# Moving a third of a head's value projection behind the sample products of the head before, and the store of V behind the copies of the keys

## The chip, the cores and the metric

The kernel runs on one core of a Trainium2 chip. The metric is the device time of one execution in microseconds, the median of several runs. The core's engines work side by side and meet at semaphores: TensorE (PE) multiplies matrices, VectorE (DVE) and ScalarE (ACT) do elementwise work, GpSimd (POOL) prepares weights, SyncE (SP) issues the transfers of weights. ACT issues transfers too.

## The reference, cut to what matters

One inference step of a two-layer trunk over a prompt of 1024 tokens and 8 sample tokens, 1032 columns in all. Layer 0 is a Mamba-2 mixer and a squared-ReLU MLP. From its output, keys and values are projected once, for 8 heads; layer 1 is differential attention over them and another MLP. For the sample tokens the attention also looks at 256 cached positions in pages. The part that the change touches, per head:

```python
kv = h @ w_kv
k = rope(kv[..., :QK_WIDTH_B].reshape(bt, l, N_HEADS_B, 2, HEAD_DIM_B), pos)
v = kv[..., QK_WIDTH_B:].reshape(bt, l, N_HEADS_B, 2 * HEAD_DIM_B)
# of a sample token: two softmaxes over 256 cached positions and its own, combined
w = (p[:, :, 0] - lam * p[:, :, 1]).astype(v_new.dtype)
o = einsum('bhqk,bkhe->bqhe', w[..., :lp], v_past) + einsum('bhqk,bkhe->bqhe', w[..., lp:], v_new)
o = rms_norm(o, subln_g) * (1.0 - lam_init)
return o.reshape(bt, l, V_WIDTH_B) @ w_o
```

Keys and values of all heads are outputs as well, and are stored from SBUF as they are (`kT`, `vT`).

## The kernel before

**Tiling.** Activations lie transposed: 128 partitions of features by 1032 columns of tokens, cut into NCH = 3 chunks of CW = 344 columns. A weight unit is 128 x 1024; SP loads it, POOL splits it into a high and a low part (`wh`, `wl`), and a product is the sum of three matmuls (high by high, high by low, low by high) so as to keep fp32 precision. One chunk of a projection over 1024 features is thus 8 x 3 = 24 matmuls of 344 columns (`chunk_of`, line 323), into one of three banks of `jb`. A bank is given back through `bank_free`, a filled bank is announced through `chunk_full`.

**The attention in passes.** `project_head(at, n, new, fin)` is written once for each engine and does two things interleaved: it begins head n (`new`: rotary queries and keys, projection of V) and ends head p = n - 1 (`fin`: the sample tokens' attention, the normalisation, the output projection by `w_o`). `attend(n)` then does the prompt's attention of head n and, between its steps, projects the queries and keys of head n + 1. Pass 0 only begins, passes 1 to 7 do both, pass 8 only ends. The order within a pass is written out by hand for each engine; nothing plans it.

**PE in a pass** (line numbers of the profile): broadcast of the sample queries (580), turn of the queries by `perm` (572), chunk 0 of V (323), sample scores transposed (590, 592), chunk 1 of V, then, after `rope_done`, turn of the keys by `perm` (572), chunk 2 of V. Then the sample tokens: after `sp_ready` the weights are spread over partitions (605, 606), after `wsm_ready` come 32 products of the cached values with one column each (612), which raise `so_full`. Then, after `osq_done`, the sums of squares over each column (377, `rms_sums`), after `raw_v` the transposes of V (622), after `orms_inv` the spread of the reciprocal roots (385, `rms_spread`), and after `a_lo` the output projection of head p (323 again, 8 jobs of 3 chunks of 3 matmuls).

**ACT in a pass**: high halves of the queries (981), exponential of the sample scores (984), the three chunks of V copied from `jb` to `raw` (`take`, 770), a drain that raises `raw_v`, the store of V (992), high halves of the keys (995), the square of `ob` (998, raises `osq_done`), copies of the key halves to the other partitions by transfers (`twin`, 970), the store of the keys (1002), the copies of the low halves (970 again, after DVE's `k_low`), the root (1007), the high part of V (1010), the high part of the output (1014).

**DVE in a pass**: sample scores (1453, 1460), rotary queries (1421 to 1426), softmax of the sample scores (1466 to 1478, raises `sp_ready`; 1481 raises `wsm_ready`), rotary keys, the sample output (1489, after `so_full`, raises `o_smp`), low halves of the keys (1439), V's sample columns (1496, after `raw_v`), the reciprocal of the root (1182), the normalisation (1503), low parts (1510, 1513), and the accumulation of the output projection (1132).

The scores of a head (655) wait until all its key copies have landed (`k_twin`). The next write into `raw` waits for the stores (`v_out`, `k_out`) in `attend`.

Of the kernel before, what the change touches and what calls it, by code (L numbers as in the profile page):

```python
# [28 lines left out]
ACT = mybir.ActivationFunctionType  # L29
# [6 lines left out]
T = SEQ + NB  # L36
NCH = 3
CW = T // NCH
KD = D // P
# [45 lines left out]
def half_of(m):  # L85

    return slice(HD * m, HD * m + HD)
# [23 lines left out]
def program(nc, a, o):  # L111
    with ExitStack() as ctx:
        def sb(name, shape, dt=F32, into=None):
            return (into or ctx).enter_context(nc.sbuf_tensor(name, shape, dt))
# [5 lines left out]
        xh = sb("xh", [P, KD, T], F32R)  # L120
        xl = sb("xl", [P, KD, T], F32R)
# [70 lines left out]
        raw = sb("raw", [P, T], F32, m)  # L192
# [60 lines left out]
        s = {n: sem(n) for n in names}  # L253
# [59 lines left out]
        def _(pe):  # L313
            mm = nc.tensor.matmul

            def chunk_of(place, c, j, kt, rh, rlo):

                slot, credits, _ = place
                pe.wait_ge(bank_free[c], credits)
                cols = slice(c * CW, (c + 1) * CW)  # L320
                for k in range(kt):
                    for w, x, p in ((wh, rh, 0), (wh, rlo, 1), (wl, rh, 2)):
                        last = mm(jb[:, c, 0:CW], w[slot][:, j * kt + k], x[:, k, cols],  # L323
                                  start=(k == 0 and p == 0), stop=(k == kt - 1 and p == 2))
                        if c == 0 and j == 0 and k == 0 and p == 0:
                            last.then_inc(unit_begun, 1)
                last.then_inc(chunk_full, 1)
# [247 lines left out]
            def project_head(at, n, new, fin):  # L575

                p = n - 1
                if fin:
                    for b in range(NB):
                        last = mm(aux[:, b // 4, (b % 4) * 128:(b % 4) * 128 + 128],  # L580
                                  smp[:, 0, b:b + 1].to_broadcast([P, P]), ident[:], start=True, stop=True)
                    last.then_inc(s["qb_full"], 1)
                if new:
                    perm_of(2 * n + 1, raw)
                    vp = (unit(at), *at.job())
                    chunk_of(vp, 0, 0, KD, xh, xl)
                if fin:

                    pe.wait_ge(s["ssc_ready"], p + 1)
                    mm(aux[0:16, 0, 256:257], qkn[:].rearrange("p m b -> p (m b)"), one[:], start=True, stop=True)  # L590
                    for g in range(PAGES):
                        last = nc.tensor.transpose(aux[0:16, 0, g * 128:(g + 1) * 128],
                                                   ssc[:, g].rearrange("p m b -> p (m b)"), ident[:])
                    last.then_inc(s["srow_full"], 1)
                if new:
                    chunk_of(vp, 1, 0, KD, xh, xl)

                    pe.wait_ge(s["rope_done"], 2 * n + 1)
                    perm_of(2 * n + 2, raw_k)
                    chunk_of(vp, 2, 0, KD, xh, xl)  # L600
                if fin:

                    pe.wait_ge(s["sp_ready"], p + 1)
                    for g in range(PAGES):
                        mm(aux[:, 1, g * 8:g * 8 + 8], srow[0:16, g * 128:(g + 1) * 128], pair[0:16, 0:8], start=True, stop=True)
                    mm(aux[:, 1, 16:24], srow[0:16, 256:257].to_broadcast([16, P]), pair[0:16, 0:8], start=True,
                       stop=True).then_inc(s["wsm_full"], 1)
                    pe.wait_ge(s["wsm_ready"], p + 1)
                    pe.wait_ge(s["pv_in"], 16 * p + 16)
                    for b in range(NB):  # L610
                        for g in range(PAGES):
                            last = mm(aux[:, 1, 32 + b:33 + b], past[:, b * PAGES + g], wsm[:, g, b:b + 1],
                                      start=(g == 0), stop=(g == PAGES - 1))
                    last.then_inc(s["so_full"], 1)
                if fin:
                    rms_sums(p, "orms_full", "osq_done", pp, 1)
                if new:

                    pe.wait_ge(s["raw_v"], n + 1)
                    pe.wait_ge(s["rope_done"], 2 * n + 2)  # L620
                    for c in range(8):
                        last = nc.tensor.transpose(aux[:, 3 + c // 4, (c % 4) * 128:(c % 4) * 128 + 128],
                                                   raw[:, c * 128:(c + 1) * 128], ident[:])
                    last.then_inc(s["vt_ps"], 1)
                if fin:
                    rms_spread(p, "orms_scale", "orms_inv")
                if fin:
                    slot = unit(at)
                    place = (slot, *at.job())
                    for c in range(NCH):  # L630
                        pe.wait_ge(s["a_lo"], 3 * p + c + 1)
                        chunk_of(place, c, 0, 1, ah, al)
                    for j in range(1, KD):
                        place = (slot, *at.job())
                        for c in range(NCH):
                            chunk_of(place, c, j, 1, ah, al)
# [93 lines left out]
        def _(act):  # L730
# [36 lines left out]
            def take(c, done, dst, func, **kw):  # L767

                act.wait_ge(chunk_full, done + c + 1)
                af(dst, jb[:, c, 0:CW], func, **kw).then_inc(bank_free[c], 1)  # L770
# [201 lines left out]
            def project_head(at, n, new, fin):  # L972
                p = n - 1
                if fin:

                    act.wait_ge(s["ssc_ready"], p + 1)
                    act.dma_start(past[:], vgat[:, :, bass.ds(p * P, P)].rearrange("g t d -> t g d")).then_inc(s["pv_in"], 16)
                if new:
                    act.wait_ge(s["rope_done"], 2 * n + 1)
                    for m_ in range(2):  # L980
                        af(q2[m_][half_of(m_)], rot[half_of(m_), 0:SEQ], ACT.Copy).then_inc(s["qk_hi"], 1)
                if fin:
                    act.wait_ge(s["snm_ready"], p + 1)
                    af(srow[0:16, 0:257], srow[0:16, 0:257], ACT.Exp, scale=SCALE, bias=st[0:16, 4:5],
                       accum_out=st[0:16, 5:6]).then_inc(s["sexp_ready"], 1)
                if new:
                    _, done = at.job()
                    for c in range(NCH):
                        take(c, done, raw[:, c * CW:(c + 1) * CW], ACT.Copy)
                    act.drain().then_inc(s["raw_v"], 1)  # L990
                    act.wait_ge(s["raw_v"], n + 1)
                    act.dma_start(o["vT"][:, bass.ds(n, 1)].rearrange("p a t -> p (a t)"), raw[:]).then_inc(s["v_out"], 16)
                    act.wait_ge(s["rope_done"], 2 * n + 2)
                    for m_ in range(2):
                        af(k2h[m_][half_of(m_)], rot[half_of(m_), 0:SEQ], ACT.Copy).then_inc(s["qk_hi"], 1)
                if fin:
                    act.wait_ge(s["o_smp"], p + 1)
                    af(pp[:, 0:T], ob[:], ACT.Square).then_inc(s["osq_done"], 1)
                if new:
                    act.wait_ge(s["qk_hi"], 4 * n + 4)  # L1000
                    twin(k2h)
                    act.dma_start(o["kT"][:, bass.ds(n, 1)].rearrange("p a t -> p (a t)"), rot[:]).then_inc(s["k_out"], 16)
                    act.wait_ge(s["k_low"], 2 * n + 2)
                    twin(k2l)
                if fin:
                    act.wait_ge(s["orms_full"], p + 1)
                    af(rstd[:, 0], aux[:, 0, 0:9], ACT.Sqrt, bias=eps[:]).then_inc(s["orms_sqrt"], 1)
                if new:
                    act.wait_ge(s["vt_ps"], n + 1)
                    af(vth[:], aux[:, 3:5].rearrange("p a (b c) -> p (a b) c", b=4), ACT.Copy).then_inc(s["vt_hi"], 1)  # L1010
                if fin:
                    for c in range(NCH):
                        act.wait_ge(s["on_ready"], 3 * p + c + 1)
                        af(ah[:, 0, c * CW:(c + 1) * CW], ob[:, c * CW:(c + 1) * CW], ACT.Copy).then_inc(s["a_hi"], 1)
                    at.job(8)
# [43 lines left out]
            _, done = at.job(2)  # L1059
# [687 lines left out]
```

## Time and profile before

| what | value |
|---|---|
| median of 3 runs | 3885.5 us (3884.25 to 3893.59) |
| span of the profiled execution | 3857.8 us |
| busy in the span | PE 89%, DVE 59%, ACT 25%, POOL 26% |
| mean granted clock of TensorE in the span | 0.922 |
| attention, passes 0 to 8 | about 2085 to 3025 us of the span |

The span runs from the first to the last instruction; the device time of a run also holds what lies around it. The granted clock is TensorE's: 1.00 is 2.4 GHz, 0.50 is 1.2 GHz, and a mean between them is a mixture of the two. A row of the timeline tells start, duration, engine, line, operation, tiles and count of merged instructions, and in brackets the idle time before and what ended it. ACTq is ACT's sequencer, which issues transfers. PE's matmuls are pipelined: the start-to-start distance is the pace, the duration of one is longer.

### The profile page before, as it was taken

What the parts mean: (1) busy time and instruction counts of PE and PEld (TensorE: products, weight loads), DVE (VectorE), ACT (ScalarE), POOL (GpSimd) and SP (SyncE); (2) the same over time, 40 slices, a digit from 0 to 9 for tenths busy, and PEclk for the clock granted to TensorE, in tenths of its full rate; (3) what the DMA queues carried; (4) which work ended last, traced back from release to release, by engine and by line L of the source; (5) the groups of instructions that cost most, each with busy time, mean ns of one, the idle gap of its engine ahead of it and who ended that gap; (6) DMA issues with size and microseconds to landing.
All of it is one profiled execution on the core that took longest, in us unless ns stands there. A gap on an engine that the chain in (4) does not pass through costs nothing.

```text
span 3857.8 us, 55382 instructions
## 1 busy us (share of the span) xinstructions
PE 3440.0 (89%) x21050; PEld 3288.6 (85%) x21050; DVE 2287.6 (59%) x3463; ACT 953.7 (25%) x2235; POOL 1011.1 (26%) x455
## 2 busy tenths in 40 slices
PE   6888988889887899999997888888886799999997
PEld 6788888888787899999996787777775799999997
DVE  6677777777776834343457666666675753333335
ACT  3333333233332311111103323222322211111112
POOL 3123132222221233343431111111110043333331
PEclk9899999999998899999997888888897699999997
DMA  4231111111110011111112111211111011111111
GB/s 165 74 110 57 46 44 42 51 39 45 43 48 34 28 44 46 49 45 50 44 50 63 59 35 49 65 60 60 60 41 41 11 50 45 45 50 44 45 48 52
DMA packets 85936, 200.29 MB, mean 52 GB/s; under 512 B 8920, under 2 KB 46808, under 8 KB 85248
## 3 DMA queue, kind: packets, MB, share of 16 engines
q1 hardware_dynamic: 35552, 139.54, 10.8%
q10 hardware_dynamic: 50224, 58.37, 4.9%
q8 instruction: 131, 2.15, 0.2%
q14 instruction: 29, 0.24, 0.0%
HBM read 166.93 MB, written 39.60 MB: 54 GB/s over the span
## 4 chain that ended last, share of the span: by engine, by line
issue 65%; PE 19%; POOLq 9%; POOL 5%; SPq 1%; DVE 0%; ACT 0%; DMA 0%; ACTq 0%; DVEq 0%
PE jb L323 18%; POOLq L298 8%; POOL wl L299 5%; SPq L273 1%; PE aux L499 0%; DMA wraw<-in_wstream 0%; ACT acc L907 0%; DVE acc L1316 0%; POOLq L306 0%; POOLq L295 0%; SPq L263 0%; SPq L269 0%; DVE lnq L1320 0%; ACT lnq L895 0%; PE aux L506 0%
## 5 line engine op out<-in xcount | busy, mean ns | idle before, releaser
L296 POOL TENSOR_TENSOR wh<-wraw,one 128x1024 fp32r<-128x1024 f32 x225 | 444.5, 1976 | 2749.5 <-PE jb L323 2275.8
L323 PE MATMUL jb<-xh,wh 128*128 128x344 f32 x2784 | 912.7, 328 | 45.9 <-issue 18.6
L323 PE MATMUL jb<-xl,wh 128*128 128x344 f32 x2784 | 899.0, 323 | 0.0
L323 PE MATMUL jb<-xh,wl 128*128 128x344 f32 x2784 | 898.1, 323 | 0.0
L1132 DVE TENSOR_TENSOR acc<-jb,acc 128x344 f32<-128x344 f32 x672 | 332.1, 514 | 457.0 <-PE jb L323 446.3
L323 PEld LDWEIGHTS jb<-xh,wh 128*128 128x128 f32 x2784 | 532.0, 191 | 54.1 <-issue 22.8
L299 POOL TENSOR_TENSOR wl<-wraw,wh 128x1024 fp32r<-128x1024 f32 x225 | 566.3, 2517 | 32.0
L323 PEld LDWEIGHTS jb<-xl,wh 128*128 128x128 f32 x2784 | 531.5, 191 | 1.6
L323 PEld LDWEIGHTS jb<-xh,wl 128*128 128x128 f32 x2784 | 531.2, 191 | 0.0
L323 PE MATMUL jb<-hh,wh 128*128 128x344 f32 x1536 | 492.3, 321 | 0.0
L323 PE MATMUL jb<-hl,wh 128*128 128x344 f32 x1536 | 491.0, 320 | 0.0
L323 PE MATMUL jb<-hh,wl 128*128 128x344 f32 x1536 | 490.5, 319 | 0.0
L1373 DVE TENSOR_TENSOR rl<-rl 128x344 f32<-128x344 f32 x192 | 158.1, 823 | 371.7 <-ACT hh L944 371.5
L942 ACT ACTIVATE rl<-jb 128x344 f32<-128x344 f32 x192 | 87.8, 457 | 1072.7 <-PE jb L323 1045.7
L323 PEld LDWEIGHTS jb<-hh,wh 128*128 128x128 f32 x1536 | 288.8, 188 | 3.4 <-DVE acc L1132 3.4
L323 PEld LDWEIGHTS jb<-hh,wl 128*128 128x128 f32 x1536 | 288.6, 188 | 0.0
L323 PEld LDWEIGHTS jb<-hl,wh 128*128 128x128 f32 x1536 | 288.1, 188 | 0.0
L1375 DVE TENSOR_TENSOR hl<-rl,hh 128x344 fp32r<-128x344 f32 x192 | 228.4, 1190 | 15.8 <-issue 2.0
L1163 DVE SCALAR_TENSOR_TENSOR ct<-pre,pg,ct 128x1024 f32<-128x1024 f32 x96 | 165.3, 1722 | 99.4 <-ACT cnew L813 90.6
L323 PE MATMUL jb<-yh,wh 128*128 128x344 f32 x384 | 136.8, 356 | 69.0 <-DVE acc L1132 51.7
L1034 ACT ACTIVATE pp<-aux,st 128x256 f32<-128x256 f32 (+7 forms) x128 | 94.1, 739 | 280.4 <-PE jb L666 158.1
L323 PEld LDWEIGHTS jb<-yh,wh 128*128 128x128 f32 x384 | 79.2, 206 | 79.5 <-DVE acc L1132 60.2
(247 smaller groups left out, 5662.9 us busy)
## 6 DMA issues: line engine op xcount, KB each, us to landing
wraw<-in_wstream SPq DMA_DIRECT2D x225, 512.0 KB, 3.3
kgat<-in_cache_k SPq DMA_DIRECT2D x16, 512.0 KB, 5.2
vgat<-in_cache_v SPq DMA_DIRECT2D x16, 512.0 KB, 6.1
pre<-in_state ACTq DMA_DIRECT2D x16, 512.0 KB, 4.2
out_ssm_s<-pre ACTq DMA_DIRECT2D x16, 512.0 KB, 3.5
past<-kgat ACTq DMA_DIRECT2D x8, 1024.0 KB, 5.9
past<-vgat ACTq DMA_DIRECT2D x8, 1024.0 KB, 5.9
acc<-in_xT SPq DMA_DIRECT2D x8, 516.0 KB, 7.0
```

Source lines behind the costliest of these rows:

```text
L273: pages = [sp.value_load(a["ptab"][0:1, k:k + 1], min_val=0, max_val=PHYS - 1) for k in range(NB * PAGES)]
L296: nc.gpsimd.tensor_tensor(wh[slot][:].rearrange("p k m -> p (k m)"), wraw[:, slot].rearrange("p k m -> p (k m)"), one[:].to_broadcast([P, ...
L298: pool.drain()
L299: nc.gpsimd.tensor_tensor(wl[slot][:], wraw[:, slot], wh[slot][:].bitcast(F32), ALU.subtract).then_inc(w_split, 1)
L323: last = mm(jb[:, c, 0:CW], w[slot][:, j * kt + k], x[:, k, cols], start=(k == 0 and p == 0), stop=(k == kt - 1 and p == 2))
L942: af(rl[:, x % 4], jb[:, x % 3, 0:CW], ACT.Relu).then_inc(bank_free[x % 3], 1)
L1034: af(pp[:, m_ * 1024:m_ * 1024 + width], src, ACT.Exp, scale=SCALE, bias=st[:, m_:m_ + 1], accum_out=st[:, 2 + m_:3 + m_]).then_inc(s["p_r ...
L1132: tt(acc[:, k, cols], jb[:, c, 0:CW], acc[:, k, cols], ALU.add).then_inc(bank_free[c], 1)
L1163: stt(ct[:, 0:SEQ], src[:, 1 + k:1 + k + SEQ], w(k), ct[:, 0:SEQ], ALU.mult, ALU.add)
L1373: tt(rl[:, x % 4], rl[:, x % 4], rl[:, x % 4], ALU.mult)
L1375: tt(hl[b][:, j, cols], rl[:, x % 4], f(hh[b][:, j, cols]), ALU.subtract).then_inc(s["h_ready"], 1)
```

## The change

In `project_head` of PE, chunk 2 of V moves from behind the turn of the keys to behind the sample products, ahead of the sums of squares. In `project_head` of ACT, two chunks of V are taken at the old place; the third take, the drain that raises `raw_v` and the store of V move behind the copies of the key's high halves and the store of the keys, ahead of the copies of the low halves. DVE, POOL and SP are unchanged, and the number of instructions is the same. In pass 0, which has no sample products, PE's order stays as it is, and only ACT's changes; pass 8 does not change.

```diff
@@ PE, project_head
                     pe.wait_ge(s["rope_done"], 2 * n + 1)
                     perm_of(2 * n + 2, raw_k)
-                    chunk_of(vp, 2, 0, KD, xh, xl)
                 if fin:
                     pe.wait_ge(s["sp_ready"], p + 1)
...
                     last.then_inc(s["so_full"], 1)
+                if new:
+                    chunk_of(vp, 2, 0, KD, xh, xl)
                 if fin:
                     rms_sums(p, "orms_full", "osq_done", pp, 1)
@@ ACT, project_head
                     _, done = at.job()
-                    for c in range(NCH):
+                    for c in (0, 1):
                         take(c, done, raw[:, c * CW:(c + 1) * CW], ACT.Copy)
-                    act.drain().then_inc(s["raw_v"], 1)
-                    act.wait_ge(s["raw_v"], n + 1)
-                    act.dma_start(o["vT"][:, bass.ds(n, 1)].rearrange("p a t -> p (a t)"), raw[:]).then_inc(s["v_out"], 16)
                     act.wait_ge(s["rope_done"], 2 * n + 2)
...
                     act.wait_ge(s["qk_hi"], 4 * n + 4)
                     twin(k2h)
                     act.dma_start(o["kT"][:, bass.ds(n, 1)].rearrange("p a t -> p (a t)"), rot[:]).then_inc(s["k_out"], 16)
+                    take(2, done, raw[:, 2 * CW:T], ACT.Copy)
+                    act.drain().then_inc(s["raw_v"], 1)
+                    act.wait_ge(s["raw_v"], n + 1)
+                    act.dma_start(o["vT"][:, bass.ds(n, 1)].rearrange("p a t -> p (a t)"), raw[:]).then_inc(s["v_out"], 16)
                     act.wait_ge(s["k_low"], 2 * n + 2)
                     twin(k2l)
```

## Rows read from the trace of the kernel before

**Rows 1.** The page: busy time by engine, and granted clock in 40 slices.
```profile
PE 3440.0 (89%) x21050; PEld 3288.6 (85%) x21050; DVE 2287.6 (59%) x3463; ACT 953.7 (25%) x2235; POOL 1011.1 (26%) x455
...
PEclk9899999999998899999997888888897699999997
```

**Rows 2.** Passes by stretch: length, busy PE, PEld, DVE, ACT, POOL, granted clock, DMA, GB/s.
```profile
2187.70:2307.30 119.60, 101.55 (x574) 93.61 (x575) 76.28 (x134) 33.81 (x72) 17.19 (x8) 0.83 0.18 53
...
2652.50:2765.20 112.70, 95.85 (x575) 88.29 (x575) 75.89 (x134) 33.87 (x72) 17.22 (x8) 0.89 0.18 56
```

**Rows 3.** Timeline of PE in pass 4: start, us, engine, line, operation, count, idle before.
```profile
2539.80 2.00 PE L572 MATMUL aux<-raw_k,perm 128*128 128x344 f32 x6 [0.56 <-DVEq L1427]
...
2542.11 0.32 PE L323 MATMUL jb<-xh,wh 128*128 128x344 f32 x1
...
2545.25 0.32 PE L323 MATMUL jb<-xh,wl 128*128 128x344 f32 x1
2545.50 0.61 PE L605 MATMUL aux<-pair,pp 16*128 16x8 f32 x4
...
2546.72 4.20 PE L612 MATMUL aux<-ssc,past 128*128 128x1 f32 x32 [0.40 <-DVEq L1482]
2554.18 4.00 PE L377 MATMUL aux<-ones,pp 128*128 128x1 f32 x18 [3.26 <-ACT pp L998]
...
2559.80 3.90 PE L385 MATMUL aux<-ident,rstd 128*128 128x128 f32 x18
```

**Rows 4.** Stretches of pass 4, columns as in rows 2.
```profile
2545.50:2549.80 4.30, 3.90 (x35) 3.82 (x34) 3.00 (x5) 0.46 (x1) 0.00 (x0) 1.00 0.30 123
2549.80:2554.20 4.40, 1.14 (x7) 1.05 (x7) 2.51 (x4) 3.17 (x3) 0.00 (x0) 0.50 0.00 0
...
2559.70:2563.40 3.70, 3.70 (x19) 3.60 (x18) 0.02 (x1) 1.02 (x1) 0.00 (x0) 0.50 0.05 13
```

**Rows 5.** Timeline of DVE in pass 4, columns as in rows 3.
```profile
2544.62 0.40 DVE L1478 TENSOR_SCALAR pp<-pp,st,pair 16x257 f32<-16x257 f32 x1
...
2551.21 0.17 DVE L1489 TENSOR_TENSOR ob<-aux,smp 128x8 f32<-128x8 f32 x1
...
2563.74 1.54 DVE L1503 SCALAR_TENSOR_TENSOR ob<-ob,subg,aux 128x344 f32<-128x344 f32 x3 [4.02 <-PE aux L385]
```

**Rows 6.** Timeline of ACT and its transfer issues in pass 4.
```profile
2545.61 0.46 ACT L770 ACTIVATE raw<-jb 128x344 f32<-128x344 f32 x1 [2.48 <-PE jb L323]
2546.36 0.37 ACTq L992 DMA_DIRECT2D out_vT<-raw  x1
...
2553.07 1.12 ACTq L970 DMA_DIRECT2D k2h<-k2h  x2
2554.29 0.55 ACTq L1002 DMA_DIRECT2D out_kT<-rot  x1
2555.58 2.30 ACTq L970 DMA_DIRECT2D k2l<-k2l  x2
2557.91 1.28 ACT L1007 ACT_TABLE_LOAD   x1 [3.78 <-issue]
2559.21 0.27 ACT L1007 ACTIVATE rstd<-aux,eps 128x9 f32<-128x9 f32 x1
```

**Rows 7.** Pass 8: PE's products in the timeline, and their stretch.
```profile
2989.90 6.95 PE L612 MATMUL aux<-ssc,past 128*128 128x1 f32 x32 [1.11 <-DMA past<-vgat]
...
2990.00:2997.00 7.00, 6.85 (x32) 6.77 (x32) 0.11 (x1) 0.00 (x0) 0.00 (x0) 0.50 0.01 2
```

**Rows 8.** Timeline of PE: matmuls of the output projection of pass 4.
```profile
2567.07 0.49 PE L323 MATMUL jb<-ah,wl 128*128 128x344 f32 x1
...
2567.93 0.49 PE L323 MATMUL jb<-ah,wl 128*128 128x344 f32 x1
```

**Rows 9.** Pass 0: PE's first score; and the stores of V: KB, median us to landing.
```profile
2112.58 0.44 PE L655 MATMUL aux<-k2h,q 128*128 128x128 f32 x1 [8.62 <-DMA k2l<-k2l]
...
out_vT<-raw ACTq DMA_DIRECT2D x8, 516.0 KB, 2.7
```

## The prediction

> **What bounds the kernel now.** I read the page first. TensorE (PE) is busy for 89% of the span, and the row of its granted clock has digits of 9 in the dense stretches and dips of 7 and 8 where the attention heads lie [rows 1]. So PE's own order and clock set the time in most of the span, but between the projections of a head there are waits. Then I cut the attention into passes, from one product of the keys with `perm` to the next (`perm_of`, line 572). A pass takes 119.6 us at a mean granted clock of 0.83, or 112.7 us at 0.89, with the same code and the same work: five such gaps could be measured, two of the first sort and three of the second [rows 2]. The reader is to see that 7 us of a pass hang on the clock alone. Last I read one pass, number 4, engine by engine [rows 3 to 6], since the passes after it repeat it, and pass 8, which projects nothing and so shows the sample products without a dense chunk ahead of them [rows 7].
>
> In pass 4 the chain is this. PE turns the keys at 2539.80, then multiplies chunk 2 of V, 24 matmuls from 2541.37 that end at about 2545.5, then the small matmuls of line 605, then the 32 sample products of line 612 from 2546.72 to 2550.92 [rows 3]. It then stands for 3.26 us until ACT has squared `ob`, and starts the sums of line 377 at 2554.18; the spread of line 385 follows at 2559.80, and DVE takes it up at 2563.74 [rows 3, 5]. The spread waits for the root, and the root does not wait for the sums alone: ACT issues the low halves of the keys until 2557.88, loads a table for 1.28 us and only then takes the root [rows 6]. The sums had ended at 2558.18, so PE and ACT arrive almost together; whatever delays either delays the output projection.
>
> **What the change takes away.** Chunk 2 stood where PE would otherwise wait for `sp_ready`. DVE writes those weights until 2545.02, and PE reached line 605 at 2545.50 [rows 3, 5]. Without the chunk PE can start there about 0.4 us earlier, no more: 0.4 us is all that is won directly, and the rest of the chunk's time, some 3.4 us of dense work up to 2545.1, becomes a wait.
>
> **What it puts in.** The 24 matmuls now stand between the products and the sums, where PE stood for 3.26 us [rows 3]. At the full clock they take 24 x 0.157 = 3.8 us (20 steps from 2542.11 to 2545.25 [rows 3]); at half clock 24 x 0.287 = 6.9 us (three steps from 2567.07 to 2567.93, in a stretch of half clock [rows 8]). So the gap hides them nearly whole at 2.4 GHz, and half of them at 1.2 GHz. Which clock they get decides the sum.
>
> **The clock of the products.** In pass 4 the granted clock was 1.00 from 2545.5 to 2549.8 and 0.50 from 2549.8 on: it fell while PE was working on the one-column products, with 3.90 us of 4.30 busy [rows 4]. These products do not hold the clock. Pass 8 has no chunk ahead of them: PE waited, did the same small matmuls, and the clock was 0.50 through all 32 products, which took 6.95 us where pass 4 took 4.20 [rows 3, 7]. After the change passes 1 to 7 look like pass 8 there, save that the keys' turn stands some 3 us ahead. The bounds are 4.2 and 6.95 us; I take 6.95, as pass 8 is the nearest row. The products start at about 2546.7 either way (the 0.4 us is used up by the small matmuls at half clock), so they end at 2553.7 instead of 2550.9.
>
> The Trainium skill, page "TensorE: Matmul & The Clock Gate", section "Loop structure matters more than you think", says that the order of the loops decides whether matmuls stay warm: back to back they do, after a long wait they go cold. It speaks both ways here, for filling the wait ahead of the sums and against opening one ahead of the products; the trace agrees on waits, but the products, which stood back to back and still lost the clock, do not follow it [rows 4].
>
> **The chunk and what follows, in pass 4.** It starts at half clock and, being dense, should win the full clock back under way, as the output projection of the same pass does; between 3.8 and 6.9 us I take the middle, 5.3, so it ends at 2559.0. Then two paths run.
> - PE: the sums start at 2559.0 instead of 2554.18. At half clock they took 4.00, at full clock about half, 2.0: done at 2561 to 2563.
> - ACT: it takes the chunk (0.1 + 0.46), drains and signals itself (2546.07 to 2546.36, 0.30), issues the store of V (0.37), then the two low halves: 1.12 us as the high halves take now, or 2.30 as now; I take 1.7. Then table 1.28, root 0.27, and 0.3 to the spread [rows 3, 6]. Together 4.8, so the spread starts at 2563.8 instead of 2559.80: 4.0 us late. ACT is the later of the two, unless the sums run at half clock.
>
> That ACT waits for the chunk is the new wait of this change: behind it in ACT's queue stand the store of V, the low halves, the root and the copy of V, and PE, DVE and the output projection wait for the root. The copies of the keys and their store now stand ahead of the take, at 2553.07 to 2554.84 [rows 6]; the square, which waits for the products, comes about 1 us later than now and takes these with it, still before 2559.0, so they cost nothing. DVE's copy out of V waits for the same signal, with nothing but the reciprocal behind it.
>
> The spread itself took 3.90 at half clock [rows 3, 4]. If the chunk has left the clock at 2.4 GHz, it takes 1.95 and the head is late by 2.0; if the clock is down again, by 4.0. Between the chunk and the spread lie 4.8 us of sums, transposes and waiting, as there did after the chunk of before, and there the clock had fallen [rows 4]. I put three spreads in four at half clock: 0.75 x 4.0 + 0.25 x 2.0 = 3.5 us a pass, for seven passes 24.5 us. The bounds of a pass are 0 (products and chunk at full clock, spread at half) and 5.6 (the chunk wholly at half clock: 1.6 more).
>
> **Pass 0** has no products, so PE's order is as before, but on ACT the take, the signal and the store (1.13 us) now stand ahead of the low halves, which had 0.74 us to spare (2554.84 to 2555.58 in pass 4) [rows 6]. PE waited 8.62 us for exactly these copies [rows 9]. At least 0.4 us; at most the 2.7 us in which a store of V lands [rows 9] on top, 3.1; I take 1.5. The skill, page "DMA: Bandwidth & Descriptors", section "Queues, rings and completion order", says that each engine takes descriptors in the order of the ring; by it the upper end, 3.1, would hold here and the sum be 1.6 us more. No run here shows such a pair yet. Later passes have the output projection between the copies and the scores. The weight queues of SP and POOL are passed by nothing: the unit of V stays in use some us longer and the next one waits for its first matmul as now.
>
> **Sum.** 24.5 + 1.5 = 26 us on the profiled execution, whose span is 3857.8 us; its device time with what lies around the span is that of the runs, with a median of 3885.5 (3884.25 to 3893.59), so I add there: 3911 us. From 0 to 5.6 us a pass, with 0.4 to 3.1 for pass 0, the sum goes from 3886 to 3928.
>
> **Rivals.**
> - *The filled wait keeps the clock up* (faster). Products at 2.4 GHz end at 2550.5, the chunk at 2554.3, and the sums and the spread run at full clock. ACT then has its root about when it has it now, and the spread saves 1.95 us: 7 x 1.95 = 13.7, less 1.5 in pass 0, gives 3873. It decides if the products still run at the full clock. For it: the chunk is dense and stands nearer to the spread. Against it: pass 8 [rows 7], and the fall during the products in pass 4 [rows 4].
> - *The loss is given back* (no change). Either products and chunk keep the clock and only the spread does not (0 a pass), or the later parts of the pass fall into the better of the two lengths of [rows 2]: two passes of 119.5 that become 112.7-like would return 14 of the 26 us. 3886 to 3897.
> - *The passes take the longer form* (much slower). The five short passes get the clock of the first two as well as the loss: 5 x 6.9 = 34.5 more, 3945. For it: two lengths exist for the same work. Against it: a shift by some us can as well lead out of the long form.
>
> **How the numbers follow.** The forecast, some 2 to 5.6 us a pass, has 0.62; given back 0.20; longer form 0.10; faster 0.08. The likeliest time is 3911 us. The range of 8 in 10 goes from 3888 to 3932: it takes in the bounds of the forecast and part of the case that gives back, and leaves out the faster one and most of the longer form. A measurement can tell some 0.3%, 11.7 us, from no change. Faster by more than that (under 3873.8): 0.07. Within (to 3897.2): 0.21. Slower: 0.72.
>
> **What would show it.** In the changed kernel: PE idle some 3 us between line 572 and line 605, ended by DVE's line 1478; the products of line 612 at near 7 us and granted clock 0.50; the first matmuls of the chunk 0.287 us apart; the sums starting some 5 us later against the keys' turn; the store of V issued just ahead of the low halves, and the root waiting for ACT's own queue. The prediction is wrong if the products stay near 4 us, if the spread takes 2 us in most passes, or if the passes keep 112.7 us.

## The result and the profile after

The changed kernel took 3892.4 us (median; 3882.0 to 3897.9) where the kernel before, measured beside it, took 3873.8 (3856.7 to 3893.6). The ratio is 1.0038, with a 95% interval of 1.0023 to 1.0053: slower, by little more than the 0.3% that can be told here. (The ratios given with an interval are not quotients of two medians, which would be 1.0048 here.) A second comparison later (e10, below) gave 1.0017 [0.9983, 1.0052]. Over all runs of this study the unchanged kernel has a mean of 3876.9 us and goes from 3847 to 3901, the changed one a mean of 3890.0, from 3879 to 3898: 13 us more, 0.34%. I had forecast 3911 in a range of 3888 to 3932. The time lies inside it and the sign is right; the size was not. One execution of e8 took 4826.9 us at a mean granted clock of 0.637, where all others lie below 3926, and is left out of its ratio.

The page of the changed kernel: busy PE, and the granted clock in 40 slices.

```profile
span 3894.8 us, 55382 instructions
...
PE 3460.2 (89%) x21050; PEld 3307.2 (85%) x21050; DVE 2286.6 (59%) x3463; ACT 952.9 (24%) x2235; POOL 1008.9 (26%) x455
...
PEclk9899999999998899999997888888887699999997
```

PE is busy 20 us longer for the same 21050 instructions [rows 1]: more of them run at the lower clock, as the stretches below show. The span also tells what lies around it: this execution took 3896.59 us, 1.8 more than its span. I come back to that number.

The passes of the changed kernel, cut from one turn of the keys to the next (columns as in rows 2; the first line is pass 0, the others are passes 1 to 4):

```profile
2103.23:2198.09 94.86, 74.06 (x431) 66.41 (x429) 59.49 (x94) 27.24 (x63) 12.86 (x6) 0.86 0.20 61
2198.09:2314.45 116.36, 98.11 (x575) 90.51 (x575) 75.93 (x134) 33.71 (x72) 17.15 (x8) 0.88 0.18 54
2314.45:2437.01 122.56, 103.32 (x575) 95.35 (x575) 76.44 (x134) 33.70 (x72) 17.20 (x8) 0.83 0.17 53
2437.01:2553.36 116.35, 98.11 (x574) 90.49 (x575) 75.92 (x134) 33.70 (x72) 17.14 (x8) 0.88 0.17 53
2553.36:2675.93 122.57, 103.35 (x575) 95.41 (x575) 76.48 (x134) 33.70 (x72) 17.22 (x8) 0.83 0.17 53
```

They alternate between 116.4 and 122.6 us. Before, two of the first six passes took 119.5 and four 112.7 [rows 2]. Each form is some 3 to 4 us longer than its counterpart.

PE in pass 3 of the changed kernel, and the spread of pass 4 (columns as in rows 3):

```profile
2437.01 2.00 PE L572 MATMUL aux<-raw_k,perm 128*128 128x344 f32 x6 [0.53 <-DVEq L1429]
2442.31 0.61 PE L604 MATMUL aux<-pair,pp 16*128 16x8 f32 x4 [3.31 <-DVEq L1481]
2443.54 6.53 PE L611 MATMUL aux<-ssc,past 128*128 128x1 f32 x32 [0.40 <-DVEq L1484]
...
2450.36 0.49 PE L323 MATMUL jb<-xl,wh 128*128 128x344 f32 x1
...
2455.78 2.06 PE L377 MATMUL aux<-ones,pp 128*128 128x1 f32 x18
...
2460.27 2.17 PE L385 MATMUL aux<-ident,rstd 128*128 128x128 f32 x18 [1.50 <-DVEq L1185]
...
2576.63 3.54 PE L385 MATMUL aux<-ident,rstd 128*128 128x128 f32 x18 [1.50 <-DVEq L1185]
```

The opened wait is there: 3.31 us ahead of the small matmuls (now line 604), ended by DVE. The products (now line 611) take 6.53 us instead of 4.20, the chunk follows them, and the sums of line 377 start 18.77 us behind the turn of the keys instead of 14.38 [rows 3]. The same in stretches, with the granted clock as the first number behind the five engines (columns as in rows 2): the small matmuls, the start of the products, their rest, the first and the last part of the chunk, and the spreads of passes 3 and 4.

```profile
2442.30:2443.50 1.20, 0.83 (x6) 0.74 (x6) 0.20 (x2) 0.00 (x0) 0.00 (x0) 1.00 0.00 0
2443.50:2444.06 0.56, 0.52 (x5) 0.53 (x5) 0.40 (x2) 0.00 (x0) 0.00 (x0) 1.00 0.00 0
2444.10:2450.00 5.90, 5.90 (x30) 5.90 (x29) 3.58 (x4) 2.11 (x2) 0.00 (x0) 0.50 0.00 0
2450.00:2454.20 4.20, 4.20 (x16) 4.20 (x16) 2.61 (x3) 1.07 (x1) 0.00 (x0) 0.50 0.64 148
2454.40:2455.80 1.40, 1.40 (x11) 1.40 (x10) 0.00 (x0) 0.00 (x0) 0.00 (x0) 1.00 0.63 257
...
2460.20:2462.50 2.30, 2.17 (x18) 2.08 (x18) 0.02 (x1) 0.65 (x1) 0.00 (x0) 1.00 0.27 93
2576.60:2580.20 3.60, 3.54 (x18) 3.44 (x18) 0.00 (x0) 0.61 (x1) 0.00 (x0) 0.58 0.16 58
```

The small matmuls still run at 2.4 GHz. Half a microsecond into the products the clock is at 1.2 GHz and stays there until the dense chunk wins 2.4 GHz back, after about three quarters of its time. In rows 4 it fell only 3 us into the products. The spread meets the full clock in pass 3 and mostly half clock in pass 4; that is the difference between 2.17 and 3.54 us.

ACT in pass 3 (columns as in rows 6), and DVE's normalisation, which takes up the spread:

```profile
2455.97 0.46 ACT L771 ACTIVATE raw<-jb 128x344 f32<-128x344 f32 x1 [4.57 <-PE jb L323]
2456.66 0.37 ACTq L1004 DMA_DIRECT2D out_vT<-raw  x1
2457.07 1.27 ACTq L971 DMA_DIRECT2D k2l<-k2l  x2
2458.38 1.28 ACT L1009 ACT_TABLE_LOAD   x1 [1.94 <-issue]
2459.67 0.27 ACT L1009 ACTIVATE rstd<-aux,eps 128x9 f32<-128x9 f32 x1
...
2462.48 1.54 DVE L1505 SCALAR_TENSOR_TENSOR ob<-ob,subg,aux 128x344 f32<-128x344 f32 x3 [2.29 <-PE aux L385]
```

The sums ended at 2457.84, but the root stands behind ACT's take, the store of V and the low halves and is taken at 2459.67: ACT's queue is the later of the two paths, as forecast. The root ends 22.93 us behind the keys' turn; before it was 19.68 [rows 3, 6]. The normalisation starts at 25.47 in the four passes with a short spread and at 26.85 in the three others, against 23.94 [rows 3, 5]: 1.5 or 2.9 us later.

What is left of a pass behind the normalisation shows a second thing. The kernel before, passes 2 and 4, from the normalisation to the next turn of the keys:

```profile
2331.39:2426.82 95.43, 81.69 (x462) 75.04 (x463) 64.96 (x115) 24.33 (x59) 17.19 (x8) 0.86 0.13 40
2563.75:2652.51 88.76, 75.53 (x462) 69.24 (x463) 64.53 (x115) 24.33 (x59) 17.20 (x8) 0.94 0.14 42
```

And the changed kernel, passes 3 and 4:

```profile
2462.48:2553.36 90.88, 77.88 (x462) 71.62 (x463) 64.63 (x115) 24.32 (x59) 17.14 (x8) 0.91 0.13 41
2580.20:2675.93 95.73, 81.74 (x463) 75.16 (x463) 65.19 (x115) 24.32 (x59) 17.22 (x8) 0.86 0.13 41
```

The same 462 or 463 matmuls take 88.8, 90.9 or 95.5 us, at a mean granted clock of 0.94, 0.91 or 0.86. So a pass is the time up to the normalisation plus one of a few tails. Most of the difference lies late in them. The same two tails of before, from 30 us behind the normalisation on:

```profile
2361.39:2426.82 65.43, 57.67 (x346) 52.96 (x345) 41.28 (x63) 17.71 (x40) 9.31 (x5) 0.90 0.11 34
2593.75:2652.51 58.76, 51.45 (x340) 47.28 (x339) 39.49 (x61) 17.24 (x39) 8.58 (x4) 1.00 0.12 37
```

There the short tail keeps the full clock and the long one does not; the middle one of pass 3 above is at 0.94. Per pass the change adds 1.5 to 2.9 us to the first part; which tail a pass draws moves as much again.

Between the two profiled executions the spans differ by 37.0 us. Of these 8.9 lie ahead of pass 0, in code that the change does not touch; 1.5 in pass 0; 26.7 in passes 1 to 6, about half ahead of the normalisation (3 x 1.5 + 3 x 2.9 = 13.2) and half in the tails; what is left cancels. That these add up to some 28 us, near the 26 that I had forecast, is luck: the profiled execution of before lies some 17 us below the mean of its runs, as is told below.

### The profile page after: what moved, and what is told of

Same layout as the page of the kernel before. It is cut to its first block, busy times and chain, and to the rows that moved or that the text cites. A ratio compares the mean times of both kernels' runs of the same rounds, so it can differ in the third digit from the quotient of the medians.

```text
span 3894.8 us, 55382 instructions
## 1 busy us (share of the span) xinstructions
PE 3460.2 (89%) x21050; PEld 3307.2 (85%) x21050; DVE 2286.6 (59%) x3463; ACT 952.9 (24%) x2235; POOL 1008.9 (26%) x455
## 4 chain that ended last, share of the span: by engine, by line
issue 65%; PE 19%; POOLq 9%; POOL 5%; SPq 1%; DVE 0%; ACT 0%; DMA 0%; ACTq 0%; DVEq 0%
PE jb L323 18%; POOLq L298 8%; POOL wl L299 5%; SPq L273 1%; PE aux L499 0%; DMA wraw<-in_wstream 0%; ACT acc L908 0%; DVE acc L1318 0%; POOLq L306 0%; POOLq L295 0%; SPq L263 0%; SPq L269 0%; DVE lnq L1322 0%; ACT lnq L896 0%; PE aux L506 0%
## 5 line engine op out<-in xcount | busy, mean ns | idle before, releaser
L323 PEld LDWEIGHTS jb<-xh,wh 128*128 128x128 f32 x2784 | 539.9, 194 | 72.7 <-issue 41.9
L323 PEld LDWEIGHTS jb<-xl,wh 128*128 128x128 f32 x2784 | 539.3, 194 | 0.9
```

## Experiments

The profiles show the mechanism but not what the parts are worth, and with tails that vary by 7 us a single pair of profiles can't. My theory: the opened wait ahead of the products costs the clock (cover theory), and the chunk's new place behind the products is in itself a gain. Rivals: the chunk's new place is the loss; or ACT's queue is; or the root's time, not the clock of the products, decides which tail a pass draws. In all runs "before" is the kernel before, measured beside the run on the same chip: e1 to e4 share one chip, e5 to e8 a second, e9 and e10 a third. Differences between runs of different chips are less certain than their ratios to "before".

### The two halves alone

```diff
 e1, the changed kernel with PE's half undone (only ACT's order is changed)
+                    chunk_of(vp, 2, 0, KD, xh, xl)          # behind perm_of(2n+2)
-                if new:                                     # behind so_full
-                    chunk_of(vp, 2, 0, KD, xh, xl)
 e2, the kernel before with PE's half alone (ACT's order is the old one)
-                    chunk_of(vp, 2, 0, KD, xh, xl)          # behind perm_of(2n+2)
+                if new:                                     # behind so_full
+                    chunk_of(vp, 2, 0, KD, xh, xl)
```

> ACT's half of the change alone: PE multiplies chunk 2 at its old place, ACT takes it late and stores V behind the keys. Theory (the chunk no longer covers the wait ahead of the sample products, so the clock falls before them and the chunk ends late): the chunk is done early, so ACT loses at most the take, the signal and the store (1.13 us) less 0.74 us of slack; root 0 to 0.5 us later in the pass (20.2 after the keys' turn instead of 19.7), products at near 4 us as before, time within 5 us of before. Rival (the longer way of V through ACT's queue is the cost, whatever PE does): root about 3 us later as in the changed kernel, time 15 to 19 us above before.

> PE's half alone: chunk 2 behind the sample products, ACT still takes it ahead of the keys' copies and of the square. Theory: the products run as in the changed kernel (6.5 us, chunk ends 18.7 us after the keys' turn), and only then come the keys' high halves (2.1), the square (1.1), the sums; root 27 to 31 us after the keys' turn instead of 22.9, 4 to 8 us a pass, time 45 to 75 us above before. Rival (only ACT's order costs): like before.

ACT's half alone gave 3867.2 us against 3881.7, a ratio of 0.9965 [0.9944, 0.9986]: 14 us faster, where I had put it within 5 us. PE's half alone gave 3921.4 against the same, 1.0110 [1.0081, 1.0138]: 40 us lost, fewer than the 45 to 75 that I had put. Two passes of e1 (columns as in rows 2):

```profile
2199.75:2313.10 113.35, 95.43 (x574) 87.68 (x575) 75.83 (x134) 33.74 (x72) 17.22 (x8) 0.89 0.18 55
2313.10:2428.87 115.77, 98.72 (x574) 91.01 (x575) 75.95 (x134) 33.73 (x72) 17.16 (x8) 0.85 0.18 55
```

The six passes of e1 take 113.0 to 115.8 us; none has the 119.5 of before. Its root ends 20.37 us behind the keys' turn, 0.7 later than before and a little more than I had put, because the take, the drain and the store of V now stand ahead of the low halves. That a later root goes with a faster kernel was new, and e5 follows it. In e2, pass 4 (keys' turn at 2564.59), PE's products and sums and the take of chunk 2:

```profile
2571.12 6.97 PE L611 MATMUL aux<-ssc,past 128*128 128x1 f32 x32 [0.40 <-DVEq L1483]
...
2583.57 0.46 ACT L771 ACTIVATE raw<-jb 128x344 f32<-128x344 f32 x1 [15.65 <-PE jb L323]
...
2588.09 3.90 PE L377 MATMUL aux<-ones,pp 128*128 128x1 f32 x18 [4.55 <-ACT pp L999]
```

With ACT's old order the take stands ahead of the high halves and the square, so ACT waits 15.65 us for the chunk and PE then waits 4.55 for the square; the sums start 23.50 us behind the keys' turn. ACT's half of the change is what takes 4.7 of these away again (18.77): without it PE's half loses 40 us.

### Cover for the products

24 matmuls of the same unit and chunk, whose results are not used, are put where chunk 2 was (e3, into the changed kernel) or where it went (e4, into the kernel before).

```diff
+            def dense(place, credits, k1=KD):
+                pe.wait_ge(bank_free[2], credits)
+                for k in range(k1):
+                    for w, x, p in ((wh, xh, 0), (wh, xl, 1), (wl, xh, 2)):
+                        mm(jb[:, 2, 0:CW], w[place[0]][:, k], x[:, k, 2 * CW:T],
+                           start=(k == 0 and p == 0), stop=(k == k1 - 1 and p == 2))
 e3, the changed kernel, behind perm_of(2n+2)
+                    if fin:
+                        dense(vp, vp[1])
 e4, the kernel before, behind so_full
+                if new and fin:
+                    dense(vp, vp[1] + 1)
```

> The changed kernel, with 24 more matmuls at the old place of chunk 2 in passes 1 to 7, into the same bank; their result is not used. Theory (the lost cover is the cost): the wait ahead of the products is filled, products take about 4 us again and end some 11 us after the keys' turn, the chunk follows at full clock for part of its way and ends at 15 to 17 instead of 18.7; root at 20 to 21.5 instead of 22.9; 1.5 to 3 us a pass less than the changed kernel, time 10 to 20 us below it, near before or under it. Rival (the chunk costs wherever it stands behind the products, through ACT's queue): root at 22.9 still, time as the changed kernel.

> The kernel before, with 24 more matmuls behind the sample products in passes 1 to 7, into a bank that is free; their result is not used. PE alone gets the dense work of the change at its new place; the cover ahead of the products and ACT's order stay. Theory: products as before (to 11 us after the keys' turn), the dense work to 15 or 17, the sums 0.5 to 3 us late but at full clock (2 us instead of 4), root within 0.5 us of before or up to 1 later, the spread sometimes at full clock (2 instead of 4); time 5 us above to 15 us below before. Rival (dense work in that wait delays the sums, the clock gives nothing back): sums end 3 us later, root 3 us later, time 15 to 20 us above before.

e3 took 3856.4 us, 0.9933 [0.9909, 0.9958] of the kernel before. It differs from the changed kernel in the cover alone, and lies 30 to 36 us below its two medians, where I had put 10 to 20: with the opened wait covered the loss is gone. In its pass 4 (keys' turn at 2547.22), the stretch of the products, then PE's sums:

```profile
2552.90:2557.90 5.00, 4.61 (x40) 4.50 (x40) 3.68 (x5) 0.00 (x0) 0.00 (x0) 0.98 0.00 0
```

```profile
2554.14 3.75 PE L621 MATMUL aux<-ssc,past 128*128 128x1 f32 x32 [0.39 <-DVEq L1494]
...
2563.14 2.06 PE L377 MATMUL aux<-ones,pp 128*128 128x1 f32 x18
```

The products run at 0.98 and take 3.75 us, the sums start 15.92 us behind the keys' turn instead of 18.77. Where the time comes from is to be read with care. The normalisation starts at 24.2 to 25.0, 0.5 to 2.6 us sooner than in the changed kernel but no sooner than before (23.94). Passes 1 to 6 are 29.9 us shorter than in the changed kernel's profile, 10.1 of them ahead of the normalisation and 19.8 in the tails: 88.5 to 91.3 us, none of 95.5. The gain on before, 25 us by the medians, does not show between the two profiles (spans of 3859.5 and 3857.8), as that of before lies some 17 us below the mean of its runs; that it lies in the tails too is argued, not shown. And 14 of the 25 came with ACT's half alone (e1, same chip), so that the chunk's new place with its cover adds 11.

e4 took 3851.3 us, 0.9923 [0.9894, 0.9952], 30 us below before where I had put 15 at most. Here the wait behind the products is filled and nothing is moved. Its pass 4 (keys' turn at 2541.95):

```profile
2559.45 2.06 PE L377 MATMUL aux<-ones,pp 128*128 128x1 f32 x18
2562.29 2.07 PE L385 MATMUL aux<-ident,rstd 128*128 128x128 f32 x18
```

The sums start 3.1 us later than before [rows 3] and yet both they and the spread run at 2.4 GHz, about 2.06 us each instead of 4.00 and 3.90, and the head ends 1.5 us sooner (normalisation at 22.45 against 23.94). In passes 1, 3 and 5 the sums start at 15.9 and the normalisation at 22.2. So filling the wait is worth some 30 us where the cover stays and ACT's order is the old one.

That any 24 more dense matmuls help, wherever they stand, would be a rival to the opened wait as the cause; the runs taken together speak against it. With ACT's new order, dense work ahead of the products alone gave 3867 (e1), behind them alone 3892 and 3886 (the change), in both places 3856 (e3). One and the same chunk costs some 20 to 25 us more at its new place than at its old one; taking the work from ahead of the products costs 30 to 36 us, and what is put behind them brings 11. e8 asks for the dose:

```diff
-                    dense(vp, vp[1] + 1)
+                    dense(vp, vp[1] + 1, 5)
```

> The kernel before with 15 instead of 24 dense matmuls behind the products (result not used). Theory (the dense work pays by what it does to the clock of sums and spread, and costs by what it delays the sums): it ends at 13.3 to 15 after the keys' turn, so the sums start at 14.4 to 15 instead of 15.9 or 17.5; if the clock still comes back in time for sums and spread, time as with 24 or up to 5 us less; if not, sums of 4 us again and time near before. The run tells which.

With 15 matmuls instead of 24 the time was 3865.6 us against 3872.4, 0.9972 [0.9938, 1.0005]: not to be told from no change. Neither branch of what I expected came: the sums run at full clock and the time stays near before. Its pass 1, in stretches: the 15 matmuls, the sums, the wait for the root, the spread.

```profile
2206.50:2210.30 3.80, 3.80 (x16) 3.79 (x16) 1.91 (x4) 3.18 (x3) 0.00 (x0) 0.55 0.03 8
2210.30:2212.40 2.10, 2.10 (x21) 2.10 (x20) 1.44 (x3) 0.00 (x0) 0.00 (x0) 1.00 1.00 224
2212.40:2215.80 3.40, 0.95 (x9) 0.72 (x7) 0.21 (x1) 1.81 (x3) 0.00 (x0) 0.65 0.94 307
2215.80:2220.00 4.20, 4.01 (x18) 3.91 (x18) 0.08 (x1) 0.66 (x1) 0.00 (x0) 0.50 0.04 12
```

The sums profit as in e4, but they end sooner while the root stays where it was; PE stands for most of 3.40 us, the clock falls there, and the spread pays it back. Here, filling the wait only in part moved it behind the next step.

### ACT's queue and the root

```diff
 e5, the kernel before: about 0.65 us of ACT work (a copy of 560 scratch columns onto themselves) ahead of the root
+                if new and fin:
+                    af(pp[:, 1100:1660], pp[:, 1100:1660], ACT.Copy)
 e6, the changed kernel; e7, e4; e9, e3: the low halves are issued behind the root
-                    act.wait_ge(s["k_low"], 2 * n + 2)
-                    twin(k2l)
                 if fin:
                     act.wait_ge(s["orms_full"], p + 1)
                     af(rstd[:, 0], aux[:, 0, 0:9], ACT.Sqrt, bias=eps[:]).then_inc(s["orms_sqrt"], 1)
+                if new:
+                    act.wait_ge(s["k_low"], 2 * n + 2)
+                    twin(k2l)
```

> The kernel before with one idle copy more on ACT ahead of the root in passes 1 to 7 (560 columns of a scratch buffer onto itself, about 0.65 us), nothing else moved. In the run with ACT's half alone the root was 0.67 us later and the time fell by 14 us. Theory A (a small delay of the root alone puts the passes into a shorter form of the clock; V's new place on ACT has no part in it): root 20.3 to 20.5 us after the keys' turn, passes of 113 to 116 us and none of 119.5, time 8 to 18 us below before. Theory B (the gain comes from V's copy and store standing elsewhere): time as before or up to 5 us above, passes of 112.7 and 119.5 mixed.

> The changed kernel with the copies of the low key halves issued behind the root instead of ahead of it. Theory (in the changed kernel ACT's queue behind the chunk sets the root: take, signal, store of V, low halves, table): root at 21.3 to 21.8 us after the keys' turn instead of 22.9, the spread as much earlier, time 3 to 12 us below the changed kernel unless the clock takes it back. Rival (the sums on PE set the root): root at 22.9 still.

e5 took 3866.2 us (3860.7 to 3875.0) against 3872.4 (3849.4 to 3900.7): 0.9990 [0.9964, 1.0017]. The verdict is mixed. A root that is only 0.7 us later does change the tails: the six passes take 113.1 to 116.0 us and none 119.5, as in e1, and the runs spread over 14 us (12 runs) instead of 51 (35 runs). But the mean did not fall by an amount that can be told. Whether e1's 0.35% has a part of its own is open. Two tails of e5, passes 1 and 2:

```profile
2213.45:2304.80 91.35, 78.27 (x462) 71.61 (x463) 65.04 (x115) 24.31 (x59) 17.20 (x8) 0.91 0.14 43
2329.42:2418.18 88.76, 75.61 (x463) 69.32 (x463) 64.56 (x115) 24.32 (x59) 17.21 (x8) 0.94 0.14 42
```

e6 took 3875.4 us, 0.9997 [0.9966, 1.0027]. It is 10 to 17 us below the changed kernel's two medians, though only the issue of two transfers moved; I had put 3 to 12. These medians are from different chips; by the ratios to before the gain is 0.2 to 0.4%, and the intervals overlap. Its pass 4 (keys' turn at 2547.38):

```profile
2566.14 2.06 PE L377 MATMUL aux<-ones,pp 128*128 128x1 f32 x18
...
2568.72 0.27 ACT L1007 ACTIVATE rstd<-aux,eps 128x9 f32<-128x9 f32 x1
2569.32 2.18 PE L385 MATMUL aux<-ident,rstd 128*128 128x128 f32 x18 [0.19 <-DVEq L1186]
```

The sums stand where they stood (18.76), the root ends at 21.62 instead of 22.93, and the spread now runs at full clock in all passes. So ACT's queue ahead of the root was a part of the changed kernel's loss. The passes still vary, from 113.0 to 119.7 us, though the normalisation starts at 24.16 in each: the tails are drawn behind it.

> The kernel before with the dense matmuls behind the products (result not used) and the copies of the low key halves issued behind the root. With the dense matmuls alone the sums ended at 18.0 or 19.6 and the root at 19.7 or 19.9. Theory: root at 18.3 to 19.9 now, up to 1.4 us earlier in every other pass, time 0 to 8 us below that run, 15 to 30 below before. Rival: the clock's forms eat it, time within 3 us of that run.

> The changed kernel with both remedies: 24 matmuls at the old place of chunk 2 (result not used) and the low key halves issued behind the root. Theory (the change costs by the lost cover and by what stands ahead of the root on ACT): sums end at 18.0 or 19.6 us after the keys' turn as with the cover alone, root at 18.8 to 20.5, time 3838 to 3856, at or below the cover alone (3856) and 35 to 55 us below the changed kernel. Rival (one remedy already gives all there is): time as with the cover alone.

e7 (nothing moved on PE, wait filled, root first) took 3844.1 us, 0.9930 [0.9900, 0.9960]; e9 (chunk moved, wait covered, root first) 3842.1, 0.9891 [0.9841, 0.9941], with the kernel before at 3891.1 beside it. By medians, from different chips, they are 2 us apart. e9 beats both kernels (the changed one took 3885.9 beside it) and has the evenest passes. That both remedies are better than the cover alone (3856.4, 0.9933) is not clear of the intervals. Pass 4 of e9, and PE in it (keys' turn at 2534.07):

```profile
2534.07:2646.70 112.63, 98.92 (x598) 91.01 (x599) 76.35 (x134) 33.83 (x72) 17.21 (x8) 0.91 0.18 56
```

```profile
2541.00 3.73 PE L621 MATMUL aux<-ssc,past 128*128 128x1 f32 x32 [0.39 <-DVEq L1495]
...
2549.99 2.06 PE L377 MATMUL aux<-ones,pp 128*128 128x1 f32 x18
...
2553.17 2.17 PE L385 MATMUL aux<-ident,rstd 128*128 128x128 f32 x18 [0.18 <-DVEq L1196]
```

Products, sums and spread all run near the full clock, the normalisation starts 21.30 us behind the keys' turn, 2.6 sooner than before, and the six passes take 112.4 to 112.6 us.

### The changed kernel again

> The changed kernel once more, beside the kernel before on the same chip. Expected: 3885 to 3900 us, passes of 116.4 and 122.5 us in turn, root 22.9 us after the keys' turn; 12 to 22 us above before.

3885.9 us (3879.4 to 3897.8), 1.0017 [0.9983, 1.0052]. The root ends at 22.92 again; the passes take 116.1 to 116.5 us four times and 122.4 to 122.5 twice, so the alternation of the first profile is not fixed, but its two forms are. The kernel before was at 3891.1 beside it, in two clusters (five runs of 3847 to 3854, twelve of 3872 to 3900), so that by the medians the changed kernel is 5 us faster here and by the means (3887.3 and 3879.1) 8 us slower; I had put 12 to 22 above. The scatter of before over 53 us, against 18 of the changed kernel, is enough to make the two comparisons differ.

## Why the prediction was partly right

**Right, step by step.** The wait of some 3 us ahead of the small matmuls (3.31); the products at half clock (6.53 for 6.95); the chunk starting at half clock and winning the full clock back (5.7 us for 5.3, ending at 18.77 for 19.2); ACT's own queue, not the sums, ahead of the root (e6 moves the root by 1.3 us). Pass 0 lost 1.5 as put (first score 19.70 us behind the keys' turn instead of 18.21), but that term was a value between two bounds, and its fit is luck. e3 shows the cause: with the wait covered the loss is gone. The rival that the filled wait keeps the clock up fell with the products' clock of 0.50, and the longer form for all passes did not come: three of the first six have the long tail, where two had it before.

The page of the Trainium skill that I weighed on the order of loops, "TensorE: Matmul & The Clock Gate", section "Loop structure matters more than you think", agrees with e3 and e4 on waits: with them filled, the products (e3) and the sums and the spread (e4) ran at or near 1.00. On the products of the changed kernel it does not, since they stood back to back for 5.9 us and stayed at 0.50.

In pass 0 my upper bound of 3.1 us put the landing of the store of V on top of the later issue; the pass lost 1.5. Of these 0.85 are the later issue of the low halves (13.36 us behind the keys' turn for 12.51), and they land 5.0 to 5.2 us after their issue instead of 4.4 to 4.7. The store of V ahead of them lands 5.1 us after its own issue there, not 2.7 as the median of before [rows 9], so it is in flight together with them and its time is not added to theirs. The Trainium skill's page "DMA: Bandwidth & Descriptors", section "Queues, rings and completion order", says that descriptors are taken in the order of the ring but that a later one may finish its write earlier; the 3.1 was my estimate, not a figure of the page.

**Mis-sized terms.** Three, and together they made the sum too large.
- The spread. I put three in four at half clock; in four of the seven passes it ran at full clock (2.17 us) and in three it took about 3.54. By my own sign (a spread of 2 us in most passes) the prediction is wrong in this. I had argued from the chunk of before, behind which the clock fell after 4.3 us [rows 4]; but there the one-column products followed it, and here, with the sums and the transposes behind it, the clock held over 4.5 us into the spread, in four passes to its end.
- ACT's chain behind the chunk: 4.5 us from the chunk's end to the spread instead of 4.8, since the two low halves took 1.27 and not 1.7.
- The chunk ended 0.4 us sooner, because the products did start 0.4 earlier (the small matmuls ran at 1.00 and not, as I had put, at half clock) and ran 0.4 faster; the chunk itself took 0.4 more.

With these the direct cost is 4 x 1.5 + 3 x 2.9 = 14.7 us, and 16 with pass 0, where I had 26. The pooled means differ by 13, the medians of the first comparison by 18.6.

**The step that failed** is the base of the sum, and in the sum the spread. I added the 26 us to the median of the three runs shown, 3885.5, and took the 27.7 us between the profiled span and it as lying around the span. The span of the changed kernel's profile and its own time are 1.8 us apart; so the profiled execution of before took some 3860 us and was another one than the three. The kernel before scatters over 54 us, and its mean over all 90 runs is 3876.9. The three runs shown lay in the upper half of these (places 57, 62 and 71 from the fastest); the profiled one would be at place 14. On that base the sum as I had it would give 3903, and the measured terms 3893, where 3892.4 and 3885.9 came. The wrong base and the oversized sum both pushed the forecast up, 9 and 10 us. Part of this fit is luck, for the sum put the tails, some 90 us of each pass, at no change and priced another only as a rival; between the two profiles they differ by 13.8 us in passes 1 to 6, about as much as the direct cost.

The rows held a warning that I read and priced only as a rival: two lengths of a pass for the same work [rows 2]. In the changed kernel they are not two sorts of pass but a draw made in each execution, as the profile of e10 shows, where other passes have the long form. Of the kernel before only one execution was profiled, some 3860 us with two long tails; at 6.7 us a tail, an estimate from these rows, it would take 3846 with none and 3893 with seven, and its runs go from 3847 at a mean clock of 0.928 to 3901 at 0.913. The rival "given back" named this, and by its number (3886 to 3897) it holds the result. Its mechanism is not borne out: no pass of the changed kernel became as short as 112.7, and against the one profile of before its tails are longer, not shorter.

**Open.** What decides which of the tails a pass draws. In the profiles of e5 and e1, one execution each, a root 0.7 us later goes with no long form, in e6 the same normalisation time is followed by all three, and in e9 the passes are even. No run here shows the rule. How a covered wait ahead of the products shortens the tails, which begin some 14 us behind them, is open with it. Whether the 8.9 us ahead of pass 0 are more than scatter was not tried; the first turn of the keys lies between 2093.5 and 2104.6 us in the kernels of this study, whose code is the same up to there.

## What to carry to other kernels

Before a dense block is moved into a later wait, ask what ran at full clock only because the block stood ahead of it: filling one wait by opening another moved the low clock from the sums to the products, and covering the opened wait (24 unneeded matmuls, e3) was worth 30 to 36 us. On an engine that also issues transfers, put the one small operation that the next engine waits for ahead of issues that have time (e6: the root came 1.3 us earlier, and the medians are 10 to 17 us lower). And compare the profiled execution with its own time, and look at the scatter of the base, before a sum of 1% is added to a median of three.

## What the runs showed of the hardware

- 32 one-column products back to back ran at a granted clock of 0.50 from half a microsecond after their start, busy for 5.90 us of 5.90; the 344-column chunk behind them won 1.00 back after some 4.3 us.
- Work that nobody needs can shorten a kernel: 168 more matmuls, 24 in each of seven passes, took 30 to 36 us off the changed kernel (e3) and 30 us off the kernel before (e4).
- The same tail of 462 matmuls takes 88.8, 90.9 or 95.5 us at 0.94, 0.91 or 0.86, from one pass to the next of one execution (e4 and e7 show 93.1 as well); in passes 1 to 6 of e9 it took 91.1 to 91.3 every time.
- The issue of the same two transfers of low halves held ACT's sequencer for 2.30 us when it came 0.7 us behind the issue of the store of the keys [rows 6], for 2.22 to 2.26 us 1.5 us behind it, with the issue of the store of V between (e1), and for 1.27 us when it came 5 us behind it and just behind the store of V.
